# Twelve conditioning chunks of the second layer computed in the two layer norm pauses, eight chunks loaded first

## What is computed

```python
def trunk(x, c, s_all, w_ada, b_ada, w_in, w_out, ...):
    c_act = jax.nn.silu(c)
    for l in range(DEPTH):                                   # DEPTH = 2
        mod = jnp.einsum('bd,de->be', c_act, w_ada[l]) + b_ada[l]
        sh1, sc1, gt1, sh2, sc2, gt2 = [m[:, None, :] for m in jnp.split(mod, 6, axis=-1)]
        h = x * (1.0 + sc1) + sh1
        y, s_new, vn = token_mixer(h, s_all[l], w_in[l], w_out[l], ...)   # projections, gMLP, HGRN2
        x = layer_norm(ALPHA * x + gt1 * y, ln1_w[l], ln1_b[l])
        h = x * (1.0 + sc2) + sh2
        f_out = swiglu(...) if l % 2 == 0 else moe_swiglu(...)
        x = layer_norm(ALPHA * x + gt2 * f_out, ln2_w[l], ln2_b[l])
```

## Time and profile before

| what | us |
|---|---|
| median of three timed runs (1614.65 to 1615.91) | 1614.83 |
| the profiled execution | 1617.73 |
| its span, first to last instruction | 1616.0 |
| projections of layer 0, first matmul to the last level | 46.70 to 217.80 |
| first matmul of the SwiGLU, after the first pause | 308.08 |
| first matmul of layer 1, after the second pause | 563.68 |
| the last level of layer 1's projections | 678.40 |

### The profile page before, as it was taken

How to read it: one execution, slowest core, us unless ns; L and a number is a source line. 1 busy time by engine, 2 the same in 40 slices (tenths; PEclk the granted TensorE clock), 3 DMA queues, 4 the chain that set the end, 5 groups by cost and what they waited for, 6 DMA issues and landing times.

```text
span 1616.0 us, 22378 instructions
## 1 busy us (share of the span) xinstructions
PE 1516.9 (94%) x8616; PEld 1277.5 (79%) x8616; DVE 1174.0 (73%) x1261; ACT 907.8 (56%) x845; POOL 62.0 (4%) x92
## 2 busy tenths in 40 slices
PE   5899998799999799988899999999999999999995
PEld 1667787699999699866788888888888888888874
DVE  2433557655566865665788988889888898888987
ACT  2444435343333365461676767677676776767762
POOL 2000010100000110002100000000000000000000
PEclk8899979899999999989999999999999999999998
DMA  9999935244444243132399999999999999999995
GB/s 322 327 353 335 349 98 158 83 158 150 140 154 148 88 151 127 53 111 66 135 354 350 358 333 358 336 347 349 335 364 329 344 348 333 363 339 366 350 362 176
DMA packets 217742, 416.06 MB, mean 257 GB/s; under 512 B 7923, under 2 KB 79773, under 8 KB 217638
## 3 DMA queue, kind: packets, MB, share of 16 engines
q1 hardware_dynamic: 214086, 402.31, 71.8%
q0 software_dynamic: 3552, 12.33, 2.6%
HBM read 407.79 MB, written 6.82 MB: 257 GB/s over the span
## 4 chain that ended last, share of the span: by engine, by line
PE 52%; DVE 5%; ACT 1%; issue 1%; DMA 1%; DVEq 0%; ACTq 0%
PE bank L665 14%; PE bank L667 14%; PE bank L666 14%; PE bank L1060 1%; PE bank L1098 1%; DVE w_lo L1582 1%; PE bank L668 1%; PE bank L670 1%; PE bank L669 1%; PE bank L765 1%; PE bank L1141 1%; PE bank L1142 0%; DMA raw_ring<-in_e_down_dram 0%; DVE w_lo L1573 0%; PE bank L1011 0%
## 5 line engine op out<-in xcount | busy, mean ns | idle before, releaser
L1582 DVE TENSOR_TENSOR w_lo<-raw_ring,w_hi 128x2048 fp32r<-128x2048 f32 x264 | 604.2, 2290 | 98.4 <-ACT w_hi L1311 97.7
L1311 ACT ACTIVATE w_hi<-raw_ring 128x2048 fp32r<-128x2048 f32 x264 | 506.7, 1919 | 231.8 <-PE bank L667 219.3
L665 PE MATMUL bank<-w_hi,xg_hi 128*128 128x512 f32 (+1 forms) x768 | 293.2, 382 | 3.0 <-DVE w_lo L1582 1.5
L667 PE MATMUL bank<-w_hi,xg_lo 128*128 128x512 f32 (+1 forms) x768 | 288.8, 376 | 0.0
L666 PE MATMUL bank<-w_lo,xg_hi 128*128 128x512 f32 (+1 forms) x768 | 288.8, 376 | 0.0
L668 PE MATMUL bank<-act_hi,w_hi 128*128 128x320 f32 x736 | 237.3, 322 | 29.2 <-DVE act_lo L1632 22.3
L669 PE MATMUL bank<-act_lo,w_hi 128*128 128x320 f32 x736 | 231.6, 315 | 0.0
L670 PE MATMUL bank<-act_hi,w_lo 128*128 128x320 f32 x736 | 231.1, 314 | 0.0
L1573 DVE TENSOR_TENSOR w_lo<-raw_ring,w_hi 128x2048 fp32r<-128x2048 f32 x65 | 148.5, 2286 | 82.4 <-ACT w_hi L1240 82.2
L668 PEld LDWEIGHTS bank<-act_hi,w_hi 128*128 128x128 f32 x736 | 142.3, 193 | 45.3 <-issue 38.9
L667 PEld LDWEIGHTS bank<-w_hi,xg_lo 128*128 128x128 f32 x768 | 144.3, 188 | 29.2
(11 more groups left out here) (329 smaller groups left out, 1916.4 us busy)
## 6 DMA issues: line engine op xcount, KB each, us to landing
raw_ring<-in_e_gate_dram SPq DMA_DIRECT2D x90, 1024.0 KB, 5.2
raw_ring<-in_e_up_dram SPq DMA_DIRECT2D x90, 1024.0 KB, 5.5
raw_ring<-in_e_down_dram SPq DMA_DIRECT2D x88, 1024.0 KB, 5.2
raw_ring<-in_w_ada_dram SPq DMA_DIRECT2D x24, 1024.0 KB, 6.8
raw_ring<-in_w_in_dram SPq DMA_DIRECT2D x24, 1024.0 KB, 7.5
st<-in_w_ada_dram SPq DMA_DIRECT2D x12, 1024.0 KB, 8.0
kdsp<-in_w_ada_dram SPq DMA_DIRECT2D x12, 1024.0 KB, 9.0
raw_ring<-in_w_ff_gate_dram SPq DMA_DIRECT2D x11, 1024.0 KB, 5.3
```

Source lines behind the costliest of these rows:

```text
L665: pe.matmul(out, xh, wh, start=start, stop=False)
L667: return pe.matmul(out, xl, wh, start=False, stop=stop)
L1311: act.activation(w_hi[:, (NSPLIT + i) % SPL, :], raw[:, s, :], ACT.Copy).then_inc(hi_ready.sem, 1)
L1582: dve.tensor_tensor(w_lo[:, r, :], raw[:, s, :], w_hi[:, r, :].bitcast(F32), ALU.subtract).then_inc(lo_ready.sem, 1)
```

## The change

Twelve of layer 1's ada chunks (36 to 47, `NEARLY` = 36, `LATE` = 6) leave the projections of layer 0: the chunks w = 5 to 10 keep two ada chunks each in place of four. Six go behind the last `sums` of the first layer norm, six behind the last `sums` of the second. They come through the four slots of the ring, each six ahead of the weight chunk that they are named for. Their copies go to the tile accT in place of wide, which the layer norm uses, and their banks are 5, 6 and 7 in turn. The third pair of each six is turned after the following block of matmuls. Apart from that, the first eight ada chunks are now loaded ahead of w 0 and w 1, and the splitting of these two moves into the modulation.

```diff
     for w in range(2, NWIN - 1):
-        if WIN_ORDER[w] // 2 in (1, 4):
-            GROUPS.update({(w, 0): 1, (w, 1): 1, (w, 2): 2})
+        tok = WIN_ORDER[w] // 2 in (1, 4)
+        if w < 5:
+            GROUPS.update({(w, 0): 1, (w, 1): 1, (w, 2): 2} if tok else {(w, 0): 2, (w, 1): 2})
         else:
-            GROUPS.update({(w, 0): 2, (w, 1): 2})
-    PER = 4
+            GROUPS.update({(w, 0): 1, (w, 2 if tok else 1): 1})
+    LATE = 6
+    NEARLY = NALL - 2 * LATE
...
+    order = [("ada", i) for i in range(8)] + [("w", 0), ("w", 1), ("ada", 8)]
     order += [("w", 2), ("ada", 9), ("w", 3), ("ada", 10), ("ada", 11)]
...
+    late = {split_index["gate", 0, 1]: NEARLY, split_index["win", 1, WIN_ORDER[2]]: NEARLY + LATE}
+    for i in range(NWIN, NSPLIT):
+        order += [("ada", late[i] + j) for j in range(LATE)] if i in late else []
+        order += [("w", i)]
...
+            if p >= NEARLY // 2:
+                return (5, 6, 7)[p % 3]
...
+        def ada_wide(p):
+
+            return wide[:] if p < NEARLY // 2 else accT[:].rearrange("p k t -> p (k t)")[:, 0:2 * CW]
...
+                if half == 0 and p == NEARLY // 2 + 1:
+                    pe.wait_ge(var_ready.sem, var_ready.at(0, 0))
...
                 sums(l, 0, KD - 2)
                 sums(l, 0, KD - 1)
                 if l == 0:
+                    for i in range(NEARLY, NEARLY + LATE):
+                        ada(i)
...
                     for m in range(KD - 4, KD):
                         sums(l, 1, m)
+                    for i in range(NEARLY + LATE, NALL):
+                        ada(i)
...
                 deviation(l, 0)
+                if l == 0:
+                    for i in range(NEARLY, NEARLY + 4):
+                        ada_rows(i)
                 modulated(l, 1, hf)
                 if l == 0:
+                    for i in range(NEARLY + 4, NEARLY + LATE):
+                        ada_rows(i)
...
                         product(c)
+                        for p in range(NEARLY // 2, (NEARLY + LATE) // 2) if c == 0 else []:
+                            ada_sums(p)
                         make_lo(at[("up", c + 1)])
```

More of the change, by code:

```diff
@@ L108, in hybrid_trunk @@
         n += cnt_
-    assert n == NALL
-    def weight_slot(i):
-        return i % 2 if i < NWIN else (i - NWIN) % RAW
-    order = [("ada", i) for i in range(6)] + [("w", 0), ("w", 1)] + [("ada", i) for i in (6, 7, 8)]
+    assert n == NEARLY
+    order = [("ada", i) for i in range(8)] + [("w", 0), ("w", 1), ("ada", 8)]
     order += [("w", 2), ("ada", 9), ("w", 3), ("ada", 10), ("ada", 11)]
-    for w in range(NWIN - 4):
-        a = PER * (w + 3)
-        order += [("ada", a), ("ada", a + 1), ("w", w + 4), ("ada", a + 2), ("ada", a + 3)]
-    a = PER * (NWIN - 4 + 3)
-    order += [("ada", i) for i in range(a, NALL)] + [("w", i) for i in range(NWIN, NSPLIT)]
+    a = ADA_A + 4
+    for w in range(NWIN - 2):
+        n = sum(c for (v, _), c in GROUPS.items() if v == w + 2)
+        order += [("ada", i) for i in range(a, a + n // 2)] + ([("w", w + 4)] if w + 4 < NWIN else [])
+        order += [("ada", i) for i in range(a + n // 2, a + n)]
+        a += n
+    late = {split_index["gate", 0, 1]: NEARLY, split_index["win", 1, WIN_ORDER[2]]: NEARLY + LATE}
+    for i in range(NWIN, NSPLIT):
+        order += [("ada", late[i] + j) for j in range(LATE)] if i in late else []
+        order += [("w", i)]
     assert sorted(i for k, i in order if k == "ada") == list(range(NALL))
-    loads, landed, times, holds = [], {}, [0] * (RAW + 2), [None] * (RAW + 2)
+    assert sorted(i for k, i in order if k == "w") == list(range(NSPLIT))
+    loads, landed, times, holds, ring = [], {}, [0] * (RAW + 2), [None] * (RAW + 2), 0
     for key in order:
-        s = weight_slot(key[1]) if key[0] == "w" else 2 + key[1] % 4
+        if key[1] < (NWIN if key[0] == "w" else NEARLY):
+            s = key[1] % 2 if key[0] == "w" else 2 + key[1] % 4
+        else:
+            s, ring = ring % RAW, ring + 1
         loads.append((key, s, holds[s]))
@@ L130, in hybrid_trunk @@
     RAW_USES = times[:RAW]
-    MOE_RAW0 = NSPLIT - NWIN
+    MOE_RAW0 = ring
     assert NR % SPL == 0 and NR % RAW == 0 and all(w % CW == 0 for _, w in EB)
@@ L695, in ada_turn @@
                 for m in range(4):
-                    last = pe.transpose(bank[ada_bank(p)][:, m * P:(m + 1) * P], wide[:, m * P:(m + 1) * P], ident[:])
+                    last = pe.transpose(bank[ada_bank(p)][:, m * P:(m + 1) * P], ada_wide(p)[:, m * P:(m + 1) * P], ident[:])
                 last.then_inc(ada_T.sem, 1)
@@ L1250, in ada_rows @@
                     act.wait_ge(ada_T.sem, p)
-                act.activation(wide[:], bank[ada_bank(p)][:, :], ACT.Copy).then_inc(ada_row.sem, 1)
+                act.activation(ada_wide(p), bank[ada_bank(p)][:, :], ACT.Copy).then_inc(ada_row.sem, 1)
             def squares(l, i, m):
@@ L1439, in _ @@
                     deviation(l, 1)
+                    for i in range(NEARLY + LATE, NALL - 2):
+                        ada_rows(i)
             act.wait_ge(rt_mm.sem, 1)
@@ L1645, in modulate @@
                                       ALU.add).then_inc(hs_ready.sem, 1)
+                    if (l, i) == (0, 0) and a < 2:
+                        make_lo(a)
                     if a and (l, i) != (DEPTH - 1, 1):
@@ L1664, in modulation @@
                 a, b = (0, 2 * KD) if part == 0 else (2 * KD, NM)
-                dve.wait_ge(ada_sum.sem, NALL // 2 if l else b * P // (2 * CW))
+                dve.wait_ge(ada_sum.sem, l * (NADA // 2) + b * P // (2 * CW))
                 bias = vecT[:, l, V_ADA + a:V_ADA + b].unsqueeze(2).to_broadcast([P, b - a, NC])
@@ L1703, in ada_turned @@
                 if (l, w) == (0, NWIN - 1):
-                    ada_sums(NALL // 2 - 1)
+                    ada_sums(NEARLY // 2 - 1)
             dve.wait_ge(first_T.sem, 1)
@@ L1758, in _ @@
                     if w == 1 and l:
+                        for p in range((NEARLY + LATE) // 2, NALL // 2):
+                            ada_sums(p)
                         modulation(l, 1)
```

15 lines of the change are left out of this document (12 added, 3 removed).

## The result

The changed kernel takes 1595.16 us (median of four runs, 1594.50 to 1596.38) against 1614.74 for the kernel before on the same chip (four runs, 1614.15 to 1615.91). The ratio is 0.988, with a 95% interval of 0.9868 to 0.9892: 19.6 us faster, where 14.7 were forecast. The forecast of 1600.1 is 4.9 us too high, and the time lies 0.8 us under the low end of the range. The profiled execution took 1594.5 us, its span 1592.7.

A forecast was written before the change was run, and what follows sets the result against it. TensorE's own work, not the loads, was taken to bound layer 0's projections. Terms -15.5 - 0.7 - 0.8 + 0.6 + 1.7 = -14.7 us took 1614.8 to 1600.1, range 1596 to 1606.5.

The forecast's parts named there:

- twelve chunks and six pairs gone, w = 5 to 10: Layer 0's projections: chunks at 1.00 us, pairs' transposes at 0.5, plus a 0.5 us wait for sums: 15.5 us less.
- start of the projections: First projection at about 45.0 instead of 46.70; a longer later wait leaves 0.7 us won, bounds 0 and 1.7.
- first pause longer: First layer norm: fifth and sixth ada chunks wait for loads, so the SwiGLU's matmuls start 1.8 us late.
- clock and third pair's transposes behind it: SwiGLU after the first pause: full instead of half clock wins 2.6 us, the third pair's transposes cost 0.6.
- second pause longer: Second layer norm: fourth to sixth ada chunks wait for loads, so layer 1's projections start 2.4 us late.
- clock behind it: Layer 1's projections after the second pause: half of the 1.4 us lost at half clock counted as won, 0.7.
- the wait near 94: Layer 0's projections: TensorE waits 2.48 us for VectorE's sum until 94.47, behind a late w_in load; forecast to grow.
- B: Rival: something else becomes the bound, in projections or pauses; gain 9 to 11 us, 1604 to 1606, both 1609; chance 0.15.
- C: Rival: loads set the pace in layer 0's projections; twelve chunks fewer save 38 us, giving 1578; chance 0.03.
- The rule of the Trainium skill: Projections at 120 to 140 us: TensorE judged by weight loads is at 75%, loads at 92%, so loads bound.
- D: Rival: loads issued within the two pauses land late, at 14.4 us; slower by 5.6 us, 1620.4; chance 0.02.
- E: Rival: no change, since TensorE waits for the weights of w = 5 to 11 instead; 1614.8; chance 0.02.

The follow-up runs named there:

- the weights ahead: Changed kernel with each thinned weight chunk's load put ahead of its two ada loads, not between them: 1594.21 us, ratio 0.9872.

## Why the prediction was right and wrong

The terms, worked out from the milestones of the two profiled executions:

| term | forecast | measured |
|---|---|---|
| twelve chunks and six pairs gone, w = 5 to 10 | 15.5 | 17.19 |
| start of the projections | 0.7 | 2.75 |
| from there to w = 5, the rest | 0 | 1.38 |
| mixer | 0 | 1.36 |
| first pause longer | -1.8 | -1.26 |
| clock and third pair's transposes behind it | 2.0 | 2.25 |
| second pause longer | -2.4 | -2.79 |
| clock behind it | 0.7 | 1.33 |
| what lies behind layer 1's projections | 0 | 1.09 |
| sum | 14.7 | 23.3 |

The sum is that of two profiled spans. The profile of before took 3.0 us more than its median, that of after 0.7 less, which makes the 19.6 of the medians. The rows that the prediction had at 0 are these. The 1.38 us lie behind the wait near 94: in the profile of before TensorE has 0.50 of its clock over 96 to 98 us, in that of after 1.00. The 1.36 and 1.09 us have no cause shown; the mixer takes 77.7 to 82.4 us over the thirteen profiles. The six terms that the prediction sized add up to 19.5 without them; that this is the 19.6 of the medians is chance, as each profile is one execution.

**The step that failed is the start.** "But the w_in chunk of 86.86 comes in the same place of a stream that is already full, and TensorE would then wait longer at 94.47. So of 1.7 us I take 0.7." The term was 0.7 and measured 2.75, and both halves of it are wrong. The start moved beyond the bound of 1.7. The modulation starts at 37.10 on ScalarE where it started at 43.84, 6.7 us earlier, and of these the two splits that now lie within it take back 4.0, less than I counted. And the later wait, which was to grow by what the start wins, did not grow (2.38 us, and 1.98 in the kernel that only loads first), since the stream was not full. The page's slices of 40 us hid it; finer stretches of the kernel before show it:

```profile
36.00:40.00 4.00, 4.00 (x20) 0.92 (x12) 1.70 (x2) 0.00 (x0) 0.00 (x0) 0.50 0.79 292
40.00:44.00 4.00, 1.17 (x8) 0.72 (x4) 3.90 (x6) 0.76 (x2) 0.00 (x0) 0.50 0.51 152
```

and those of the changed kernel:

```profile
36.00:40.00 4.00, 0.00 (x0) 0.00 (x0) 3.08 (x5) 3.97 (x5) 3.32 (x5) 0.88 0.99 343
40.00:44.00 4.00, 0.05 (x1) 0.08 (x1) 3.27 (x4) 3.45 (x6) 0.42 (x1) 0.50 0.92 291
```

The loads stand still for lack of slots just where the start is late. SyncE's waits from 30 to 60 us in the kernel before name VectorE's splits of w 0 and w 1, whose slots w 2 and w 3 take:

```profile
SPq L446 <- DVE w_lo L1573: 12.5, 2, 11.3
```

From 51.16 on (53.59 before) each load is issued 2.4 us earlier. These slots come free as TensorE and the splits go on, so an earlier start moves the loads with it: SyncE issues the load of w = 5 at 73.32 in place of 75.75, and ScalarE starts the split of 86.86 at 84.32. The profiles with the early loading alone and with the move alone (43.90 and 46.92) put these 2.8 us on the loading.

**The term for the chunks was mis-sized, its mechanism right.** Each w from 5 to 10 became shorter by 2.7 to 2.8 us (w = 9, which also loses the wait, by 3.4), where 2.5 were named. Two chunks are 2.0 of it, as forecast. The rest is what the prediction rounded to 0.5. In w = 8 to 10 a pair stood twice between two single chunks; the row of the second operation gives the end of the transposes (TensorE before, w = 8):

```profile
165.22 0.66 PE L696 MATMUL bank<-ident,wide 128*128 128x128 f32 x4
165.81 1.06 PE L685 MATMUL bank<-raw_ring,cT 128*32 128x512 f32 x8
...
171.53 0.66 PE L696 MATMUL bank<-ident,wide 128*128 128x128 f32 x4
172.11 1.07 PE L685 MATMUL bank<-kdsp,cT 128*32 128x512 f32 x8
```

In the changed kernel the one pair that is left is followed by split matmuls:

```profile
152.89 0.66 PE L713 MATMUL bank<-ident,wide 128*128 128x128 f32 x4
153.30 0.39 PE L683 MATMUL bank<-act_hi,w_hi 128*128 128x320 f32 x1
```

So 0.59 and 0.58 turn into 0.41, which saves 0.76 where I had 0.5. In w = 5 to 7, where four chunks stood in three places and two now stand in two, the pair that goes is one of 0.58, and 48 split matmuls run unbroken in 5.83 us instead of 3.03 + 2.95: another 0.15 for the interruption. With the wait of the sum, 0.66 in its place in the timeline, this is 12 x 1.00 + 3 x 0.73 + 3 x 0.77 + 0.66 = 17.2, the measured term.

**The first pause** went as laid out: four chunks without a wait, two waited for, the third pair's transposes behind the first block. It grew by 1.26, just under the lower end of the start that was forecast (309.5 to 310.2, which is 1.4 to 2.1 late), and the layer norm was not delayed (modulation 6.59 us behind the last of the sums, 6.54 before). The half clock went, and SwiGLU plus transposes won 2.25 where 2.0 were forecast. That the clock is the cause is shown by the idle matmuls: 2.74 and 2.76 with nothing else changed. Over all profiles the price varies: with the first pause idle at its end the SwiGLU takes 244.7 to 246.2 us (four kernels), behind the idle matmuls 243.4 (two), so 1.3 to 2.8 us. With six chunks it is 243.9 (seven profiles), the third pair's transposes included.

**The second pause**: the fourth chunk's load was issued at 530.26, its slot freed by the split of w 1 (527.95 + 2.29), and that chunk began 5.1 us later, as forecast. The fifth came 3.7 us behind the fourth in place of 2.7. The two weight loads issued from 534.07 on may have slowed it; no run takes them away. The clock, of which half was counted as won, is a matter of the execution: 12.20 us and 113.39 in one, 14.01 and 113.80 in the other. The kernel's spread of 1592.9 to 1599.2 holds this 2.2 us difference.

**The rivals.** B did not come: no wait took the place of the removed work in the projections, and the pauses grew by 1.26 and 2.79 us with no half clock behind them. C's mark was a last level at 180; it stands at 196.48. The rule of the Trainium skill (Perfetto Trace Analysis, Identifying the Most-Contended Engine) that judges TensorE by its weight loads fails on this case: by it TensorE had 15% room at 140 to 160 (16.91 of 20 us), yet it never paused there, with the DMA share at 0.67, and each microsecond of its work taken away was a microsecond won. D's mark was landings of 11.6 us; from issue to use the first load of a pause took 5.2 and 5.1 us, the last 7.1 and 8.6. E's was a last level at 217.

**The range.** A repeat on another chip gave 1596.08, within it by 0.1. The distance to the range's end is small beside the spread of the changed kernel (1592.88 to 1599.20). The forecast itself was 4.9 us off: 2.05 of this are the start, which came out at four times its size, and 1.69 the chunks. That the terms for the pauses came out near what was measured (-0.47 for both with their clock, where -1.5 was forecast) is in part the luck of the execution: the repeat lost 1.8 us more in the second pause.

## What to carry to other kernels

Before a stream of loads is called full, read its share in stretches as fine as the event that you move: a mean of 40 us hid 8 us at shares of 0.79 and 0.51, and with them the fact that the loads were following TensorE's start. What a removed piece is worth is read from the distances between starts around it, and what stands behind the pieces that stay counts too: a pair of transposes cost 0.58 us ahead of an ada chunk and 0.41 ahead of a split matmul. A pause of another engine's making has room for the chunks that are loaded before its own work ends: here four (9.5 us, unchanged). The ones behind pay for a landing. Six chunks save 8.5 to 8.9 us in the projections and lengthen a pause by 1.3 to 4.6, so moving them pays; whether the fifth and sixth pay by themselves is not shown: against the kernel before on the same chip the ratio is 0.9888 with four in each pause and 0.988 with six.

## What the runs showed of the hardware

An idle TensorE costs time twice. 7.31 us of meaningless matmuls in each of the two pauses of 9.4 us make the same program 2.2 us faster (2.1 to 5.3 by the interval); this is the clock: 0.50 over 308 to 312 behind the pause without them, full behind it with them. The Trainium skill (TensorE: Matmul & The Clock Gate, Part 1: The HAM clock gate) puts it as "the default state is throttled, and activity releases the throttle"; these runs agree. What I had not expected is how far it differs between executions of one kernel: at the same place, with waits of 2.66 and 3.19 us, one had full clock throughout and the other 0.50 for a whole 4 us. The length of the wait alone does not decide it: with the move alone TensorE waited 2.50 us there and with the weights ahead 2.44, and both had half clock. And the price was in two places that a wait as such does not show: the ada chunks themselves (1.94 for 1.06 us), on the path, and in three profiles a stretch 16 to 22 us behind the second pause, which hid the second pause's gain in the run with 32 idle matmuls.

Left open: where the late stretch comes from; whether the half clock near 94 to 98 us, which all four profiles with the late start have and two of the nine with the early start, goes because of the earlier start; and why both kernels with the weights ahead have the shortest mixer (77.74 us, 79.1 to 82.4 in the others). Nothing was run on any of these.
